# Layer 0's query, key and value products in two passes over the depth, the modulation products spread anew, gates through memory

## The chip, the cores and the metric

One core of one Trainium2 chip (trn2) runs the kernel. The metric is the device time of one execution in microseconds, from first to last instruction of the core with what lies around it. The kernel before took 1590.33 us, the median of 3 runs (1589.23 to 1595.4).

## The reference

Two blocks of layers over x, 256 tokens by 2048 (fp32). All times are those of three attention-like layers, which the kernel numbers 0, 1 and 2.

- Every layer first makes modulation vectors from a condition vector: `mod = silu(c) @ w_mod + b_mod`, split in shift, scale and gate of 2048 each. There are 11 such vectors of 2048: shift, scale, gate for layer 0; shift, scale, gate for layer 1; shift and scale for the shared keys and values; shift, scale, gate for layer 2. Each costs a matrix of 2048 by 2048, 16.8 MB, for one vector times matrix.
- Layer 0: `h = rms_norm(x) * (1 + scale) + shift`; `proj = h @ w_in` (2048 by 7168) gives q, k, v for 8 dilated attention heads, q, k, v for 4 retention heads, and gates z. The heads' output is multiplied by `silu(z)`, goes through `w_out` and is added as `x + gate * out`. An RMS norm follows.
- Layer 1: differential attention with its own q, k, v, g projection (2048 by 8192) and output projection, then `layer_norm(alpha * x + gate * y)`.
- Layer 2: keys, values and forget gates from `kv_w_2`, queries and gates from `b_w_in_2`, forgetting attention, output projection and the last layer norm.

## The kernel before

**Products.** All projections run through one frame. A chunk is 512 output columns. A step is two k-tiles (256 rows) of one chunk, 128x1024 fp32 values, 512 KB from memory; a chunk has 8 steps and a pair is two chunks, 16 steps. There are 29 pairs, 464 steps. For each step SyncE loads `raw` (four slots, line 450), ScalarE casts it to `w_hi` (line 823), VectorE subtracts to get `w_lo` (line 1120), and TensorE does three products for each k-tile and half of the tokens (lines 629 to 631: high by high, low weight by high, high weight by low), 12 matmuls of 512 columns in a step. `w_hi` and `w_lo` have four slots (LEAD): ScalarE may cast step n only when TensorE has done step n-4, and SyncE may load a slot only when `w_lo` of the step four earlier is written. A chunk accumulates in two PSUM banks, one for each half of the tokens. ScalarE copies a finished chunk out (line 844 and others) and TensorE goes on in the other two banks.

**The head.** Pairs 0 and 1 (steps 0 to 31) are special, because the activations themselves depend on modulation vectors. x is loaded, squared, scaled and turned by TensorE (line 562). Then, for each of the 16 k-tiles, VectorE makes one tile of the shift and one of the scale product (line 1134: a 128x2048 tile of the modulation matrix, 1 MB, times the condition row, summed along the row), finishes them (lines 1141, 1146), ScalarE makes `act_hi` of that k-tile (1005, 1009), VectorE `act_lo` (1153), and TensorE multiplies this one k-tile with columns 0 to 2047 of `w_in`: q and k of the dilated heads, 4 chunks in all 8 PSUM banks at once (lines 578 to 580). So each k-tile of the head uses two steps of weights (1 MB) and two modulation tiles (2 MB).

**The modulation products.** 176 tiles (11 vectors by 16), in order. GpSimd issues their loads (line 505) into a ring: 6 slots in the head (`gw` and parts of `area`), 2 slots after it. A slot is free when VectorE has used it. `MOD_STEPS` gives by hand how many tiles VectorE does in each pair after the head: 8 in each of pairs 2 to 5, then 7, 6, 3 in pairs 6, 7, 8; 4, 6, 6 in pairs 9 to 11; 5, 6, 5, 8, 8 in pairs 12 to 16; 6, 4, 6, 5, 6, 5 in pairs 17 to 22 and 4 in each of pairs 23 to 26.

**The order.** Pair 2: v of the dilated heads. Pair 3: q, k of retention; four decay tables and a lambda are made beside it (lines 1488 to 1510), from twelve small loads that SyncE issues between the weights of pair 2 (line 443). Pair 4: v of retention, and the attention steps of layer 0 begin (`ATTENTION_PAIR`), woven between steps up to pair 6. Pairs 5 and 6: the gates z, which ScalarE takes through silu and VectorE multiplies in (line 1201). Then the heads' output is turned (line 609) and pairs 7 and 8 are the output projection: VectorE multiplies each chunk by the gate row, adds it to x and takes norm statistics (lines 1214, 1219, 1223). The norm (1329 or 1331) and the next turn follow. Layer 1 has pairs 9 to 18 and layer 2 pairs 19 to 28, in the same way.

**The gate row** is the layer's gate vector on all 128 partitions. In pairs 7, 17 and 27 TensorE spreads it: 16 products of a broadcast column with the identity in 4 groups (line 598), each group copied out by ScalarE (line 906).

**Queues.** SyncE issues weights and small loads, GpSimd the modulation tiles, ScalarE bias tables and norm rows. Every engine runs its instructions in the order written; each wait holds all behind it on its engine.

## Time and profile before

| what | value |
|---|---|
| median of 3 runs | 1590.33 us |
| the profiled execution's own time | 1595.93 us |
| its span | 1594.1 us |
| mean granted TensorE clock | 0.970 |
| TensorE busy | 1461.7 us (92%) |
| VectorE busy | 1173.3 us (74%) |
| ScalarE busy | 719.0 us (45%) |
| moved by DMA | 445.68 MB, mean 280 GB/s |

The profile gives, for one execution, the busy time of each engine, groups of equal instructions, and for idle time the engine or transfer that ended it. TensorE's matmuls overlap in the pipeline, so its rate is read from starts, not from the duration of one. "Granted clock" 1.00 is 2.4 GHz and 0.50 is 1.2 GHz.

### The profile page before, as it was taken

Reading aid. Unit: us, or ns where it says so; the run is one execution under the profiler, and the core shown is the slowest. Engines: PE = TensorE matmul, PEld = TensorE weight load, DVE = VectorE, ACT = ScalarE, POOL = GpSimd, SP = SyncE. Lnnn points to the kernel's source line nnn. Section 1 sums busy time; section 2 is a strip of 40 time slices with the busy share of each in tenths; the row PEclk is TensorE's granted clock in tenths of the full one; section 3 lists DMA queues with packets and bytes.
Section 4 is the critical chain, followed back from the end, with each engine's and each line's share of the span. In section 5 each row is a group of like instructions: output and inputs, shape, how many; then the busy total and the mean of one; then the engine's idle time right before and its main releaser. Section 6 shows DMA issues by size and latency. Waiting matters only on the chain.

```text
span 1594.1 us, 19384 instructions
## 1 busy us (share of the span) xinstructions
PE 1461.7 (92%) x6730; PEld 1205.5 (76%) x6730; DVE 1173.3 (74%) x1451; ACT 719.0 (45%) x1006; POOL 112.0 (7%) x211
## 2 busy tenths in 40 slices
PE   4778999998999799999999989969999999999895
PEld 3566777787788688888887867858888778888784
DVE  5997787785778778777678867877876775556456
ACT  4345355553443444344555643434443455554431
POOL 1110000001000000000001100000000000000000
PEclk8999999999999899999999999989999999999998
DMA  9998998986968389999888869839997586655552
GB/s 386 418 416 305 360 317 331 356 289 219 326 242 299 132 310 336 319 345 325 310 277 289 264 243 339 279 118 364 321 353 277 195 294 224 205 173 164 185 187 90
DMA packets 153871, 445.68 MB, mean 280 GB/s; under 512 B 11328, under 2 KB 13632, under 8 KB 130112
## 3 DMA queue, kind: packets, MB, share of 16 engines
q1 hardware_dynamic: 125136, 249.33, 44.9%
q0 software_dynamic: 25488, 185.61, 31.8%
q10 hardware_dynamic: 3168, 9.70, 1.6%
q8 instruction: 48, 0.79, 0.2%
...
## 4 chain that ended last, share of the span: by engine, by line
PE 62%; DVE 16%; DMA 13%; ACT 5%; issue 4%; ACTq 0%; DVEq 0%; SPq 0%; POOL 0%
PE bank L629 18%; PE bank L631 18%; PE bank L630 18%; DMA raw<-in_w_in 5%; DVE gw L1134 5%; DVE w_lo L1120 4%; DMA raw<-in_a_w_out 2%; DMA gw<-in_t_ada 2%; DMA raw<-in_kv_w 2%; PE bank L747 2%; ACT w_hi L823 2%; PE bank L695 2%; PE bank L609 1%; DVE area L1134 1%; DVE w_lo L1126 1%
## 5 line engine op out<-in xcount | busy, mean ns | idle before, releaser
L823 ACT CAST w_hi<-raw 128x1024 fp32r<-128x1024 f32 x464 | 485.1, 1051 | 722.1 <-PE bank L631 415.0
L1120 DVE TENSOR_TENSOR w_lo<-raw,w_hi 128x1024 fp32r<-128x1024 f32 x428 | 517.9, 1222 | 311.9 <-ACT w_hi L823 309.5
L629 PE MATMUL bank<-w_hi,act_hi 128*128 128x512 f32 x1728 | 695.1, 402 | 14.9 <-DVE w_lo L1120 9.9
L631 PE MATMUL bank<-w_hi,act_lo 128*128 128x512 f32 x1728 | 677.2, 392 | 0.0
L630 PE MATMUL bank<-w_lo,act_hi 128*128 128x512 f32 x1728 | 676.3, 391 | 0.0
L629 PEld LDWEIGHTS bank<-w_hi,act_hi 128*128 128x128 f32 x1728 | 327.4, 189 | 88.0 <-DVE w_lo L1120 16.5
L631 PEld LDWEIGHTS bank<-w_hi,act_lo 128*128 128x128 f32 x1728 | 326.4, 189 | 70.3
L630 PEld LDWEIGHTS bank<-w_lo,act_hi 128*128 128x128 f32 x1728 | 327.4, 189 | 65.4
L1134 DVE CUSTOM_DVE_ANT_0 gw<-gw,c_act 128x2048 f32<-128x2048 f32 x156 | 356.2, 2286 | 27.5 <-DMA gw<-in_t_ada 12.4
L505 POOL DMA_DIRECT2D gw<-in_t_mod x96 | 51.1, 532 | 831.0 <-DVE products L1134 820.6
L578 PE MATMUL bank<-w_hi,act_hi 128*128 128x512 f32 x128 | 54.1, 422 | 31.1 <-DVE act_lo L1153 31.1
L578 PEld LDWEIGHTS bank<-w_hi,act_hi 128*128 128x128 f32 x128 | 25.7, 201 | 41.9 <-issue 36.8
L580 PE MATMUL bank<-w_hi,act_lo 128*128 128x512 f32 x128 | 52.6, 411 | 0.0
L579 PE MATMUL bank<-w_lo,act_hi 128*128 128x512 f32 x128 | 52.5, 410 | 0.0
L1126 DVE TENSOR_TENSOR w_lo<-raw,w_hi 128x1024 fp32r<-128x1024 f32 x36 | 43.7, 1219 | 7.2 <-ACT w_hi L823 7.2
L1134 DVE CUSTOM_DVE_ANT_0 area<-area,c_act 128x2048 f32<-128x2048 f32 x20 | 45.0, 2286 | 0.0
L944 ACT ACTIVATE probs<-probs,neg_max 128x128 f32<-128x128 f32 (+1 forms) x80 | 36.6, 458 | 17.0 <-DVE neg_max L1447 16.9
L695 PE MATMUL bank<-qk_t 128*128 128x256 f32 (+1 forms) x160 | 37.7, 343 | 0.0
L609 PE MATMUL bank<-ident,resid 128*128 128x128 f32 x96 | 15.5, 323 | 23.0 <-DVE resid L1331 12.8
L747 PE MATMUL bank<-area,probs_t 128*128 128x128 f32 (+1 forms) x208 | 33.5, 299 | 0.0
L1302 DVE TENSOR_TENSOR act_lo<-bank,act_hi 128x512 fp32r<-128x512 f32 x24 | 16.0, 689 | 22.8 <-ACT act_hi L887 22.8
L609 PEld LDWEIGHTS bank<-ident,resid 128*128 128x128 f32 x96 | 14.0, 169 | 24.8 <-DVE resid L1331 13.3
...
## 6 DMA issues: line engine op xcount, KB each, us to landing
gw<-in_t_mod POOLq DMA_DIRECT2D x96, 1024.0 KB, 7.5
raw<-in_a_w_in SPq DMA_DIRECT2D x128, 512.0 KB, 6.0
...
gw<-in_t_kv_mod POOLq DMA_DIRECT2D x32, 1024.0 KB, 7.7
...
gw<-in_t_ada POOLq DMA_DIRECT2D x28, 1024.0 KB, 8.3
area<-in_t_ada POOLq DMA_DIRECT2D x20, 1024.0 KB, 10.4
```

What stands on the lines that cost most here:

```text
L578: nc.tensor.matmul(dst, hi, w_hi[:, n % LEAD, c], start=(kt == 0), stop=False)
L579: nc.tensor.matmul(dst, hi, w_lo[:, n % LEAD, c], start=False, stop=False)
L580: last = nc.tensor.matmul(dst, lo, w_hi[:, n % LEAD, c], start=False, stop=(kt == KT - 1))
L629: nc.tensor.matmul(dst, hi, w_hi[:, b, k], start=(kt == 0), stop=False)
L630: nc.tensor.matmul(dst, hi, w_lo[:, b, k], start=False, stop=False)
L631: last = nc.tensor.matmul(dst, lo, w_hi[:, b, k], start=False, stop=(kt == KT - 1))
L695: last = nc.tensor.matmul(s_bank[:, c0:c1], q[:, tt * P:(tt + 1) * P], k[:, 0:c1 - c0], start=True, stop=(layer != 2))
L747: last = nc.tensor.matmul(o_bank[:, tt * w:(tt + 1) * w], pt[:, at:at + P], area[:, V, j, c:c + w], start=(j == 0), stop=(j == keys - 1))
L823: nc.scalar.copy(w_hi[:, b], raw[:, j % SLOTS]).then_inc(hi_ready, 1)
L1120: nc.vector.tensor_tensor(w_lo[:, j % LEAD], raw[:, j % SLOTS], w_hi[:, j % LEAD].bitcast(F32), ALU.subtract).then_inc(lo_ready, 1)
L1126: nc.vector.tensor_tensor(w_lo[:, j % LEAD], raw[:, j % SLOTS], w_hi[:, j % LEAD].bitcast(F32), ALU.subtract).then_inc(lo_ready, 1)
L1134: nc.vector.tensor_tensor_reduce(out=w, in0=w, in1=c_act[:], scale=1.0, scalar=0.0, op0=ALU.mult, op1=ALU.add, accum_out=products[:, b, k: ...
```

## The change

1. **Two passes.** The head now does k-tiles 0 to 7 only (16 steps, same four chunks in 8 banks). What it has is copied by ScalarE to `area` as partial sums. Steps 16 to 39 do k-tiles 0 to 7 of six more chunks (v of the dilated heads, v, q and k of retention), 4 steps each, their partial sums copied out too. Meanwhile VectorE makes the shift and scale tiles of k-tiles 8 to 15, two in every three steps. Steps 40 to 79 do k-tiles 8 to 15 of all ten chunks; VectorE adds each to its partial sum (`add_part`, one 128x512 instruction for each half of the tokens, in place of ScalarE's copy). The number of steps is unchanged (80 up to the end of pair 4), and so is the number of matmuls.
2. **Modulation tiles spread anew.** `PAIR_TILES` replaces `MOD_STEPS`; three slots after the head (two before), five in it (six before), and from tile 15 on three. The tiles are loaded as two halves of 4 KB in each partition (one of 8 KB before).
3. **Gates through memory.** The gate part of the modulation matrices is permuted on the host so that `mod[:, gate]` stored from SBUF is the row in order; GpSimd stores it to a DRAM tensor and ScalarE loads it back broadcast to 128 partitions. TensorE's and ScalarE's parts of the spreading are gone.
4. **Weights as one stream.** The host lays all weights out in the order of the steps, so that a step is one contiguous block with 4 KB in each partition (two rows of 2 KB before, outside the head). SyncE has one loop in place of ten.
5. Smaller: the first two weight steps are loaded before the first modulation tiles; the silu of the second condition vector moves from the start of pair 4 to pair 5, next to the silu of the gates; the small loads go with steps 32 to 43; `squares` has one buffer in place of two; `w_forget` lies in `probs`.

```diff
-GEMV_RING = 2
-HEAD_RING = 6
+GEMV_RING = 3
+HEAD_RING = 5
-MOD_STEPS = {ADA_GATE: ((2, 8), (3, 8)), A_SHIFT: ((4, 8), (5, 8)),
...
+PAIR_TILES = {3: 6, 4: 8, 5: 7, 6: 8, 7: 9, 8: 10, 9: 7, 10: 7, 11: 7, 12: 7, 13: 7, 14: 3, 15: 3, 16: 3, 17: 4,
+              18: 5, 19: 7, 20: 7, 21: 7, 22: 6, 23: 5, 24: 4, 25: 4, 26: 3}
+HALF_KT = KT // 2
+SHORT = STEPS // 2
+FIRST_PAIR = 3
+HEAD_STEPS = 2 * HALF_KT
+HEAD_TILES = 2 * KT
+FIRST_ORDER = (4, 5, 8, 9, 6, 7)
+SECOND_ORDER = (6, 7, 0, 2, 4, 1, 3, 5, 8, 9)
+SECOND_AT = HEAD_STEPS + SHORT * len(FIRST_ORDER)
+FRONT_STEPS = SECOND_AT + SHORT * len(SECOND_ORDER)
+    if pair == 5:
+        return [(at, first + i) for i, at in enumerate((0, 2, 9, 10, 12, 13, 15))]
+    return [(1 + i * (13 / n), first + i) for i in range(n)]
+        def row_slot(g):
+            return g % HEAD_RING if g < 3 * HEAD_RING else g % GEMV_RING
...
         @block.sync
-            sp.wait_ge(gw_landed[0], 16)
+            for k in range(FRONT_STEPS):
+                if k == 2:
+                    sp.wait_ge(gw_landed[1], 16)
+                wait(sp, lo_ready, k - SLOTS + 1)
+                load_step(k * P, k)
+                if 0 <= k - SMALLS_AT < SMALLS:
+                    small_load(k - SMALLS_AT)
...
+            with sp.Fori(0, WEIGHT_CHUNKS) as i:
                 for j in range(STEPS):
+                    k = FRONT_STEPS + j
+                    sp.wait_ge(lo_ready, i * STEPS + (k - SLOTS + 1))
+                    load_step(i * (STEPS * P) + k * P, j)
...
         @block.gpsimd
+                if b - 1 in GATES and k == GEMV_RING - 1:
+                    store_gate(GATES.index(b - 1))
+            def store_gate(layer):
+                pool.wait_ge(mod_ready, GATES[layer] - 1)
+                pool.dma_start(gate_rows[layer].rearrange("(p k) -> p k", p=P), mod[:, GATES[layer]]
+                               ).then_inc(gate_stored, 16)
+            pool.wait_ge(raw_landed[1], 16)
...
         @block.tensor
-            def spread_gate(layer, n):
...
+            def short(n):
+                q, kt0, m, j = short_of(n)
+                if j == 0 and kt0 == 0:
+                    pe.wait_ge(parted, 2 * (m + 1) if m < 2 else 8 + 2 * (m - 1))
+                elif j == 0 and m < 2:
+                    pe.wait_ge(parted, 8 + 2 * (len(FIRST_ORDER) - 1 + m))
+                elif j == 0:
+                    pe.wait_ge(evacuated, 2 * (m - 1))
+                if kt0 and m == 0:
+                    pe.wait_ge(head_hi, kt0 + STEP_KT * (j + 1))
+                    pe.wait_ge(head_lo, kt0 + STEP_KT * (j + 1))
+                pe.wait_ge(lo_ready, n + 1)
...
         @block.scalar
-            def gate_row(layer, n):
-                act.wait_ge(t_ready, T[("gate", layer, n)] + 1)
-                nc.scalar.copy(area[:, K, 0, n * CHUNK:(n + 1) * CHUNK], t_bank[:]).then_inc(t_free, 1)
+            def gate_rows_of(layer):
+                act.wait_ge(weighed, OUT0[layer] + OUTS[layer])
+                act.wait_ge(gate_stored, 16 * (layer + 1))
+                act.dma_start(area[:, K, 0], row_of(gate_rows[layer])).then_inc(gate_landed, 16)
+            def keep_part(n):
...
+                for q in chunks:
+                    act.wait_ge(half_used, n + 1)
...
+                    for tt in range(TT):
...
+                        nc.scalar.activation(part(q, tt), bank[:], ACT.Copy, scale=part_scale(q)).then_inc(parted, 1)
         @block.vector
+            def add_part(n):
+                q, kt0, place, j = short_of(n)
+                if not kt0 or j < SHORT - 1:
+                    return
+                dve.wait_ge(half_used, n + 1)
+                for tt in range(TT):
...
+                    nc.vector.scalar_tensor_tensor(out=dst, in0=bank, scalar=part_scale(q), in1=first, op0=ALU.mult,
+                                                   op1=ALU.add).then_inc(evacuated, 1)
+            def front():
+                for m in range(HEAD_STEPS, FRONT_STEPS + LEAD):
+                    n = m - LEAD
...
+                    split_low(m, m % LEAD)
+                    kt, late = divmod(m - HEAD_STEPS, 3)
+                    if kt < HALF_KT and late < 2:
+                        gemv_step(2 * (HALF_KT + kt) + late)
+                        if late:
+                            head_finish(HALF_KT + kt)
+                    if late == 2 and 0 <= kt - 1 < HALF_KT:
+                        head_low(HALF_KT + kt - 1)
```

## Rows read from the trace of the kernel before

**Rows 1.** The page's first part: busy time, share, instructions.
```profile
PE 1461.7 (92%) x6730; PEld 1205.5 (76%) x6730; DVE 1173.3 (74%) x1451; ACT 719.0 (45%) x1006; POOL 112.0 (7%) x211
```

**Rows 2.** Busy time by stretch; then clock, DMA share, GB/s; first busy (x) is PE.
```profile
29.00:171.80 142.80, 119.55 (x480) 94.00 (x481) 127.58 (x150) 61.48 (x78) 14.78 (x28) 0.95 0.96 373
171.80:308.20 136.40, 125.94 (x545) 100.40 (x545) 108.39 (x133) 67.99 (x92) 12.12 (x23) 0.96 0.94 350
...
434.00:545.00 111.00, 100.77 (x464) 84.38 (x462) 82.19 (x93) 42.39 (x50) 5.46 (x10) 0.93 0.73 258
...
765.00:934.00 169.00, 165.03 (x778) 136.24 (x776) 131.79 (x223) 95.28 (x186) 18.57 (x34) 0.99 0.83 282
```

**Rows 3.** Busy time by stretch: steady products, and part of the head.
```profile
600.00:740.00 140.00, 140.00 (x619) 115.95 (x619) 106.69 (x93) 59.68 (x64) 10.03 (x19) 1.00 0.93 328
100.00:120.00 20.00, 16.22 (x64) 12.61 (x63) 19.60 (x25) 8.46 (x11) 2.81 (x6) 0.91 1.02 417
```

**Rows 4.** PE's waits: whole run, then 171.8 to 308.2 us. Total, times, longest.
```profile
PE bank L578 <- DVE act_lo L1153: 31.1, 15, 8.0
...
PE bank L629 <- DVE w_lo L1120: 8.4, 9, 2.6
```

**Rows 5.** Timeline of DVE, one k-tile of the head (start, duration).
```profile
34.73 1.22 DVE L1126 TENSOR_TENSOR w_lo<-raw,w_hi 128x1024 fp32r<-128x1024 f32 x1
...
36.40 1.22 DVE L1126 TENSOR_TENSOR w_lo<-raw,w_hi 128x1024 fp32r<-128x1024 f32 x1
37.53 2.28 DVE L1134 CUSTOM_DVE_ANT_0 area<-area,c_act 128x2048 f32<-128x2048 f32 x1
...
39.74 2.29 DVE L1134 CUSTOM_DVE_ANT_0 area<-area,c_act 128x2048 f32<-128x2048 f32 x1
...
42.35 1.22 DVE L1126 TENSOR_TENSOR w_lo<-raw,w_hi 128x1024 fp32r<-128x1024 f32 x1
```

**Rows 6.** Timeline, start of the head: SyncE's, ScalarE's and TensorE's rows.
```profile
14.62 1.85 SPq L461 DMA_DIRECT2D raw<-in_w_in  x4
...
26.30 1.04 ACT L823 CAST w_hi<-raw 128x1024 fp32r<-128x1024 f32 x1 [2.62 <-DMA raw<-in_w_in]
...
29.16 0.76 PE L578 MATMUL bank<-w_hi,act_hi 128*128 128x512 f32 x1 [7.98 <-DVE act_lo L1153]
```

**Rows 7.** DVE's groups, 171.8 to 308.2 us: busy, mean ns, idle before and releasers.
```profile
L1120 DVE TENSOR_TENSOR w_lo<-raw,w_hi 128x1024 fp32r<-128x1024 f32 x42 | 50.6, 1221 | 16.9 <-ACT w_hi L823 16.8
L1134 DVE CUSTOM_DVE_ANT_0 gw<-gw,c_act 128x2048 f32<-128x2048 f32 x22 | 50.4, 2290 | 13.6 <-DMA gw<-in_t_ada 11.0 <-DMA gw<-in_t_mod 2.6
```

**Rows 8.** DVE's groups, 487.4 to 541 us (pair 8 and norm).
```profile
L1219 DVE SCALAR_TENSOR_TENSOR resid<-resid,side 128x512 f32<-128x512 f32 x6 | 3.8, 683 | 0.0
```

**Rows 9.** Timeline of PE: two of the twelve gate groups, and the one that waited.
```profile
457.45 1.05 PE L598 MATMUL bank<-ident,mod 128*128 128x128 f32 x8
...
461.08 1.05 PE L598 MATMUL bank<-ident,mod 128*128 128x128 f32 x8
...
972.77 1.13 PE L598 MATMUL bank<-ident,mod 128*128 128x128 f32 x8 [1.63 <-ACT area L906]
```

**Rows 10.** Timeline of PE: first turns after norm 0, layer 1's gating, norm 1.
```profile
541.26 3.68 PE L609 MATMUL bank<-ident,resid 128*128 128x128 f32 x16 [10.17 <-DVE resid L1329]
...
940.78 3.67 PE L609 MATMUL bank<-ident,area 128*128 128x128 f32 x16 [6.87 <-DVE area L1201]
...
1053.05 3.68 PE L609 MATMUL bank<-ident,resid 128*128 128x128 f32 x16 [12.84 <-DVE resid L1331]
```

**Rows 11.** Timeline of ACT: the casts before those two waits of layer 1.
```profile
935.09 1.04 ACT L823 CAST w_hi<-raw 128x1024 fp32r<-128x1024 f32 x1 [5.47 <-DMA raw<-in_a_w_out]
...
1043.04 1.04 ACT L823 CAST w_hi<-raw 128x1024 fp32r<-128x1024 f32 x1 [4.41 <-DMA raw<-in_kv_w]
```

**Rows 12.** DMA issues of the page: KB each, median us to landing.
```profile
gw<-in_t_mod POOLq DMA_DIRECT2D x96, 1024.0 KB, 7.5
...
area<-in_final_gain ACTq DMA_DIRECT2D x1, 1024.0 KB, 8.0
```

More of the change, by code:

```diff
@@ L93, with short_of @@
 VECS = VEC_FINAL + 3 * KT
+GATES = (ADA_GATE, A_GATE, B_GATE)
 def gemv_steps(pair):
-    for b, steps in MOD_STEPS.items():
-        k = 0
-        for p, n in steps:
-            if p == pair:
-                first = 1
-                return [(first + i * ((14 - first) / n), b, k + i) for i in range(n)]
-            k += n
-    return []
+    n = PAIR_TILES.get(pair, 0)
+    first = HEAD_TILES + sum(k for p, k in PAIR_TILES.items() if p < pair)
+    if pair == 5:
+        return [(at, first + i) for i, at in enumerate((0, 2, 9, 10, 12, 13, 15))]
+    return [(1 + i * (13 / n), first + i) for i in range(n)]
+def short_of(n):
+    if n < SECOND_AT:
+        m, j = divmod(n - HEAD_STEPS, SHORT)
+        return FIRST_ORDER[m], 0, m, j
+    m, j = divmod(n - SECOND_AT, SHORT)
+    return SECOND_ORDER[m], HALF_KT, m, j
 def alibi(n):
@@ L159, in t_uses @@
                         uses.append(("probs", layer, s - 2))
-                if pair == OUT_PAIR[layer] and h < 4:
-                    uses.append(("gate", layer, h))
+                if pair == OUT_PAIR[layer] and h == 0:
+                    uses.append(("end", layer))
         if pair == FORGET_PAIR:
             uses += [("forget_rows",), ("forget",)]
-    return {u: n for n, u in enumerate(uses)}
+    count = {}
+    n = 0
+    for u in uses:
+        count[u] = n
+        n += u[0] != "end"
+    return count
 def two_blocks(nc, a, out):
@@ L530, in loads_after @@
                 for h in range(PAIR_STEPS):
-                    for at, b, k in steps:
-                        if h <= at < h + 1 and KT * b + k + GEMV_RING < MODS * KT:
-                            load(KT * b + k + GEMV_RING)
+                    for at, g in steps:
+                        if h <= at < h + 1 and g + GEMV_RING < MODS * KT:
+                            load(g + GEMV_RING)
                     if steps_of(pair, h):
@@ L780, in _ @@
             head()
-            first_pair()
-            pairs(3, 1)
+            for n in range(HEAD_STEPS, PAIR_STEPS * ATTENTION_PAIR[0]):
+                short(n)
             attention_pair(4)
@@ L966, in values_step @@
                     for tt in range(TT):
-                        nc.scalar.activation(squares[:, tt],
+                        wait(act, squared, TT * HEAD_ROOTS["head", layer, u] + tt)
+                        nc.scalar.activation(squares[:],
                                              o_bank[:, tt * WIDE:(tt + 1) * WIDE], ACT.Square,
@@ L1176, in head @@
                     head_keep(r)
-                for kt in range(KT):
+                for kt in range(HALF_KT):
                     split_low(2 * kt, 2 * kt % LEAD)
@@ L1513, in _ @@
             head()
-            for n in range(LEAD):
-                split_low(HEAD_STEPS + n, n)
-            for p in range(FIRST_PAIR, 5):
-                pair(p)
+            front()
             pair(5, gate_y(0))
@@ new lines, in weight_steps @@
+def weight_steps(inputs):
+    w_in = np.asarray(inputs["w_in"])[0]
+    out = np.empty((FRONT_STEPS + WEIGHT_CHUNKS * STEPS, P, STEP_KT * CHUNK), np.float32)
+    head = w_in[:HALF_KT * P, :4 * CHUNK].reshape(HALF_KT, P, 2, 2 * CHUNK)
+    out[:HEAD_STEPS] = head.transpose(0, 2, 1, 3).reshape(HEAD_STEPS, P, 2 * CHUNK)
+    for n in range(HEAD_STEPS, FRONT_STEPS):
+        q, kt0, _, j = short_of(n)
+        row, col = (kt0 + STEP_KT * j) * P, q * CHUNK + (0 if q < 6 else 2 * D - 6 * CHUNK)
+        step = w_in[row:row + STEP_KT * P, col:col + CHUNK].reshape(STEP_KT, P, CHUNK)
+        out[n] = step.transpose(1, 0, 2).reshape(P, STEP_KT * CHUNK)
+    at = FRONT_STEPS
+    for name, col, chunks in WEIGHT_RUNS:
+        w = np.asarray(inputs[name]).reshape(D, -1)[:, col:col + chunks * CHUNK]
+        w = w.reshape(STEPS, STEP_KT, P, chunks, CHUNK).transpose(3, 0, 2, 1, 4)
+        out[at:at + chunks * STEPS] = w.reshape(chunks * STEPS, P, STEP_KT * CHUNK)
+        at += chunks * STEPS
+    return out.reshape(-1, STEP_KT * CHUNK)
```

305 lines of the change are left out of this document (157 added, 148 removed).

## The prediction, made before the changed kernel ran

> **What bounds the kernel now.** I read the page's busy times first [rows 1]: TensorE works 92% of the span, so the kernel is near TensorE's own time and a gain must come from its idle time (132 us), from a low clock, or from work taken off it. Then busy time by stretch. Undisturbed, TensorE does 619 matmuls in 140.00 us [rows 3]: 0.2262 us each, 2.71 us for a step of 12, 21.7 us for a chunk, with VectorE at 76% and the DMA engines at 0.93. The stretches show where it is not so [rows 2]. From 29.0 to 171.8 us it does the first 40 steps, 480 matmuls, in 142.8 us; alone they take 108.6. From 171.8 to 308.2 us it does the next 40 (with 65 small products of attention) in 136.4 us and idles for 10.5.
>
> Third, what ends the waits. In the head it is `act_lo`, fifteen times, 31.1 us [rows 4], and `act_lo` is late because VectorE is full: 19.60 of 20 us [rows 3]. One k-tile takes VectorE from 34.73 to 42.35 us, 7.62 us [rows 5]: two splits of weights (1.13 us from start to start), two modulation products (2.21 us) and small work, where TensorE needs 5.4. The DMA engines are full too, 417 GB/s at share 1.02. Between 171.8 and 308.2 us it is `w_lo` that is late [rows 4], and VectorE itself waits there, 16.8 us for casts and 13.6 us for modulation tiles not yet landed [rows 7], at DMA share 0.94 and only 350 GB/s. So the head is bound by VectorE and DMA together, the stretch behind it by late transfers, and the rest by TensorE but for short waits at turns and norms [rows 10].
>
> **The change part by part**, from the profiled execution's own 1595.9 us.
>
> *Start.* The first weights are issued at 14.62 us, after the first modulation tile; the second cast waits 2.62 us for them, and the first product of the head comes at 29.16 us [rows 6]. Now two weight steps are issued at the beginning. Bounds: nothing (the 1 MB tiles then land later) and the whole wait with the one before it, some 4 us. Nearest is the wait seen: -3 us.
>
> *Steps 0 to 39.* Products and splits are the same in number, 32 and 40, but all 40 steps now share the products. VectorE needs 16 x 7.62 = 121.9 us and 8 more splits x 1.13 = 9.0: 130.9 us, in place of 142.8. In the new stage three steps cost it 8.75 us and TensorE 8.1, so VectorE still leads, narrowly. Transfers: 373 GB/s x 142.8 us = 53.3 MB [rows 2] at the head's 417 GB/s are 127.8 us, so VectorE binds, narrowly again. The copies of partial sums are ScalarE's, busy for 61 of 143 us. Bounds: 0 (the rate of the next stretch, below) and -15 (transfers alone). With some unevenness: -10 us.
>
> A rule against this part: the Trainium skill, page "DMA: Bandwidth & Descriptors", section "Where 436 GB/s comes from", says that for transfers from HBM the HBM side, about 358 GB/s a core, is what binds. By it 53.3 MB would take 149 us and the part would give nothing. The trace disagrees, with 417 GB/s in the head [rows 3].
>
> *Steps 40 to 79.* Here 14 modulation tiles are left of 22. TensorE's work is 136.4 less 10.5 us idle less 4% of clock (0.96, 5.5 us) = 120.4 us. Transfers fall from 350 x 136.4 = 47.7 MB by 8 MB to 39.3 MB, 319 GB/s, under the 328 at which TensorE never idled [rows 3]. VectorE takes over the ten chunks' sums, 20 x 0.683 = 13.7 us by the nearest instruction [rows 8]; with 40 splits (45.2), 14 products (30.9) and its other work (108.4 - 50.6 - 50.4 = 7.4) that is 97 us of 120: hidden. Without that cover it would cost its 13.7 us. What is late next: the first attention steps and the table work, 3 us by guess from two waits over 1 us left. Bounds 0 and -16: -13 us.
>
> *Gates.* Two groups start at 457.45 and 461.08 us [rows 9], 3.63 us apart with a step of 2.71 between: 0.92 us a group, 12 groups, 11.0 us, and the wait of 1.63: -12.7 us, all on TensorE. The new row is a broadcast load of 1 MB on ScalarE's queue like the gain row, which lands in 8.0 us [rows 12]; it is issued at the end of pair 6 and wanted a turn and a chunk (over 21.7 us) later. GpSimd's store waits for `mod_ready` with tile loads queued behind it, but just after VectorE has finished that vector. Both at nothing; if late, the add of the first chunk of pair 7 waits.
>
> *Pairs 7 and 8* now have 9 and 10 tiles for 6 and 3. In the first chunk of pair 8 lie six: VectorE needs 8 x 1.13 + 6 x 2.21 + 6 x 0.683 = 26.4 us against 21.7, and transfers of 18.9 MB in 43.4 us would be 435 GB/s. So it comes 4.7 us late to its last sum, and norm 0, which all wait for, moves by what is not caught up. Room there is in the time before, with DMA share 0.73 [rows 2]. Bounds 0 and +10: +3 us.
>
> *Layer 1.* Pairs 14 to 16 have 9 tiles for 21. TensorE idles 4.0 us of 765 to 934 at clock 0.99 [rows 2]: -2. The turn after the gating waits 6.87 us, norm 1 12.84 where norm 0 waits 10.17 [rows 10]; before both a cast was held 5.47 and 4.41 us by weights [rows 11]. Lighter pairs and weights in 4 KB pieces should bring them earlier: -2.5 each. Bounds 0 and -13.
>
> *At nothing:* the moved silu (ScalarE has room, and the waits at pair 4 are counted above), single `squares`, small loads (same steps), more tiles in pairs 9 to 13 (7 x 2.21 + 16 x 1.13 = 33.6 of 43.4 us), pairs 5 and 6, all of layer 2 (bounds +3 and -5).
>
> Sum: -3 - 10 - 13 - 12.7 + 3 - 7 = -42.7, so 1553.2 us for a profiled execution. This one was 5.6 us above the median of its kind; against the median it is 1547.6, rounded 1548.
>
> **Rivals.**
> - *Transfers stay slow.* The stretch behind the head moved 350 GB/s at share 0.94, 372 at a full share. If the 4 KB halves of the modulation tiles fare like that, 53.3 MB take 143 us and steps 0 to 39 give nothing: 1558. For: nothing shows 4 KB alone. Against: the head's weights have 4 KB rows already and run within the 417. The skill's 358 GB/s (same page and section) would be this case, a little worse. 0.14.
> - *Pairs 7 and 8 clog.* Both queues at 435 GB/s is above anything seen; if weights come late too, TensorE loses what VectorE does: +8 more, 1556. 0.14.
> - *The waits of steps 40 to 79 stay.* They are then the order on ScalarE and VectorE (table loads, the lambda, sums now in the way) and not transfers: 1561. Against: 13.6 us of VectorE's waits name modulation tiles [rows 7]. 0.08.
> - *The change doesn't do what it says*: all three together and no gain at the start and in layer 1, so that the gates' -12.7 stand against +3 and +8 in pairs 7 and 8: 1589. 0.04.
> - *Slower: weights late behind deeper modulation.* With three slots one more tile of 1 MB can stand in front of each weight step, 2.5 us at 417 GB/s. In pairs 9 to 13 and 19 to 21, now 7 tiles each, TensorE never idled, but share was 0.93. If its 128 steps each lost 0.5 us, 64 us: 1612. It decides from 0.33 us a step (42.7/128). Against: only 328 GB/s are asked there, a tile lands in 7.5 us [rows 12] and is used every 6.2, so seldom is more than one or two under way. 0.04.
>
> Of that last rival the Trainium skill, same page, section "Queues, rings and completion order", says that each DMA engine takes turns between queues packet by packet; smaller pieces of modulation tiles would then leave weights a larger share. No row here separates it.
>
> **How the numbers follow.** The forecast has 0.56. Its own range is 1536 to 1558. For 8 in 10 I take the good ends of start, steps 0 to 79 and layer 1 (-4 - 15 - 16 - 12.7 - 13 = -60.7, 1530) and on the other side two of the rivals together (1548 + 10 + 13 = 1571): 1528 to 1572. A measurement of this kernel can tell about 0.5%, 8 us, from no change. Faster: forecast and the first three rivals, 0.92. Same: 0.04. Slower: 0.04.
>
> **What would show it.** First product of the head near 26 us. Step 40 begins near 159 us and step 80 near 282 (171.8 and 308.2 before), the new stage at about 8.8 us for three steps with DMA near 415 GB/s. No `w_lo` waits over 1 us between them beyond two or three. The projection chunks of pairs 7, 17, 27 shorter by 3.7 us. Norm 0's wait of 10 to 15 us, norm 1's near 10, layer 1's gating near 4. It is wrong if the share is 1.0 at 370 GB/s in the front, if TensorE idles in pairs 9 to 13, or if norm 0's wait passes 20 us.

## The result, and the profile after

The changed kernel takes 1574.46 us (median of 4 runs, 1571.09 to 1577.23), the one before 1592.87 (4 runs, 1589.23 to 1596.68): ratio 0.988, 95% interval 0.985 to 0.991. So it is faster by 18 us, where 42 were forecast, and 2 us outside the range. The profiled executions differ by 21.4 us (1574.56 and 1595.93); the steps below are held against these. Of the kernels tried below, weights2k has one slow execution (a lower granted clock, 1605 us, and it is the profiled one) and respread two; the ratios leave these out, and without them the medians are 1588.5 and 1577.9 us.

The page's first part after, to set beside [rows 1]:

```profile
PE 1444.3 (92%) x6634; PEld 1190.2 (76%) x6634; DVE 1183.0 (75%) x1471; ACT 710.8 (45%) x992; POOL 113.4 (7%) x214
```

TensorE has 96 matmuls fewer (the gates' twelve groups of eight, [rows 9], are gone) and is busy 17 us less, VectorE 10 us more (the sums of the halves). Busy time by stretch, the columns as in [rows 2]: the first 40 steps, the next 40, chunks 15 and 16 (pairs 7 and 8), chunk 17 with norm 0, and chunks 39 to 41 (pairs 19 and 20):

```profile
27.80:157.60 129.80, 115.58 (x480) 92.16 (x481) 122.79 (x145) 64.57 (x88) 15.64 (x28) 0.97 1.00 402
157.60:277.90 120.30, 118.63 (x545) 97.82 (x545) 101.22 (x137) 60.23 (x81) 7.43 (x14) 1.00 0.89 326
435.40:482.50 47.10, 44.98 (x194) 35.61 (x192) 43.94 (x45) 16.34 (x16) 4.77 (x9) 1.00 0.93 359
482.50:528.10 45.60, 26.57 (x113) 20.95 (x113) 40.58 (x49) 13.48 (x17) 4.42 (x8) 0.85 0.87 347
1052.20:1129.50 77.30, 70.31 (x290) 55.96 (x289) 62.85 (x55) 29.16 (x31) 6.36 (x12) 0.96 0.89 334
```

The front does what it should: 142.6 us became 129.8 and 136.4 became 120.3, and between steps 40 and 79 TensorE idles 1.7 us of 120.3. The third and fourth row are new: there VectorE is at 93% and 89% and the DMA engines at 0.93 and 0.87, and two chunks last 47.1 us where 43.5 are needed. The turns of [rows 10] after, from the timeline of TensorE (idle time before in brackets), with the three longest of the waits inside pairs 7, 8 and 20:

```profile
498.26 0.50 PE L674 MATMUL bank<-w_hi,act_hi 128*128 128x512 f32 x1 [2.94 <-DVE w_lo L1187]
...
523.93 3.68 PE L654 MATMUL bank<-ident,resid 128*128 128x128 f32 x16 [13.84 <-DVE resid L1439]
...
919.71 3.29 PE L654 MATMUL bank<-ident,area 128*128 128x128 f32 x16 [4.50 <-DVE area L1318]
...
1023.44 3.67 PE L654 MATMUL bank<-ident,resid 128*128 128x128 f32 x16 [10.11 <-DVE resid L1441]
...
1100.14 0.50 PE L674 MATMUL bank<-w_hi,act_hi 128*128 128x512 f32 x1 [1.89 <-DVE w_lo L1187]
1125.07 0.80 PE L674 MATMUL bank<-w_hi,act_hi 128*128 128x512 f32 x1 [3.99 <-DVE w_lo L1187]
```

Norm 0's wait grew from 10.17 to 13.84 us, which is 3.7 of the 9.4 us that chunk 17 lost; in the rest of that chunk TensorE idles 5 us more and is busy 1 us more. Layer 1's gating wait fell from 6.87 to 4.50, norm 1's from 12.84 to 10.11.

Where the time went shows best in the length of each chunk. The table is worked out: the start of every 96th product of TensorE's timeline (eight steps of twelve), and the difference to the next. Bare, a chunk is 21.7 us; chunk 17 holds norm 0 and its turn, and chunks 28 to 33 attention.

| chunks | before | after | light_loads | light_vector | light_both | rear |
|---|---|---|---|---|---|---|
| 15, 16 (pairs 7, 8) | 43.7 | 47.1 | 44.8 | 46.5 | 43.5 | 48.8 |
| 17 (pair 8, norm 0) | 36.2 | 45.6 | 43.8 | 45.8 | 36.3 | 44.9 |
| 38 to 41 (pairs 19, 20) | 89.6 | 101.9 | 90.9 | 91.4 | 89.8 | 90.9 |
| lead over before at chunk 10 | | 30.3 | 30.3 | 29.6 | 30.8 | 29.3 |
| lead at chunk 18 | | 17.3 | 26.8 | 18.8 | 34.2 | 17.9 |
| lead at chunk 42 | | 17.3 | 30.0 | 16.6 | 40.1 | 25.6 |

After 80 steps the changed kernel leads by 30.3 us. It loses 5.0 in pairs 5 and 6, the gates give 4.9 in the first chunk of pair 7, and so it leads by 30.1 at chunk 15; at the end of pair 8 by 17.3. Pairs 14 to 18 bring it to 29.6, and pairs 19 and 20 take it back to 17.3.

### The profile page after: what moved, and what is told of

Same layout as the page of the kernel before. It is cut to its first block, busy times and chain, and to the rows that moved or that the text cites. A ratio compares the mean times of both kernels' runs of the same rounds, so it can differ in the third digit from the quotient of the medians.

```text
span 1572.7 us, 19098 instructions
## 1 busy us (share of the span) xinstructions
PE 1444.3 (92%) x6634; PEld 1190.2 (76%) x6634; DVE 1183.0 (75%) x1471; ACT 710.8 (45%) x992; POOL 113.4 (7%) x214
## 3 DMA queue, kind: packets, MB, share of 16 engines
q1 hardware_dynamic: 69840, 249.33, 43.5%
## 4 chain that ended last, share of the span: by engine, by line
PE 51%; DVE 20%; DMA 16%; issue 6%; ACT 6%; ACTq 0%; DVEq 0%; SPq 0%; POOL 0%
DMA raw<-in_t_steps 13%; PE bank L674 13%; PE bank L676 13%; PE bank L675 13%; DVE gw L1201 8%; DVE w_lo L1187 5%; ACT w_hi L873 3%; PE bank L797 2%; DVE w_lo L1193 2%; PE bank L745 2%; PE bank L640 1%; PE bank L642 1%; PE bank L641 1%; PE bank L654 1%; DMA gw<-in_t_mod 1%
## 5 line engine op out<-in xcount | busy, mean ns | idle before, releaser
L676 PE MATMUL bank<-w_hi,act_lo 128*128 128x512 f32 x1536 | 602.0, 392 | 0.0
L675 PE MATMUL bank<-w_lo,act_hi 128*128 128x512 f32 x1536 | 601.2, 391 | 0.0
L1201 DVE CUSTOM_DVE_ANT_0 gw<-gw,c_act 128x2048 f32<-128x2048 f32 x170 | 388.3, 2285 | 5.0 <-DMA gw<-in_t_ada 3.5
L674 PEld LDWEIGHTS bank<-w_hi,act_hi 128*128 128x128 f32 x1536 | 290.6, 189 | 86.2 <-DVE w_lo L1187 21.4
L676 PEld LDWEIGHTS bank<-w_hi,act_lo 128*128 128x128 f32 x1536 | 290.1, 189 | 62.6
L675 PEld LDWEIGHTS bank<-w_lo,act_hi 128*128 128x128 f32 x1536 | 290.7, 189 | 58.1
L1193 DVE TENSOR_TENSOR w_lo<-raw,w_hi 128x1024 fp32r<-128x1024 f32 x84 | 102.1, 1222 | 25.6 <-ACT w_hi L873 25.4
L529 POOL DMA_DIRECT2D gw<-in_t_mod x96 | 51.5, 536 | 696.9 <-DVE products L1201 690.7
L642 PE MATMUL bank<-w_hi,act_lo 128*128 128x512 f32 x256 | 99.8, 390 | 0.0
L641 PE MATMUL bank<-w_lo,act_hi 128*128 128x512 f32 x256 | 99.7, 390 | 0.0
L640 PEld LDWEIGHTS bank<-w_hi,act_hi 128*128 128x128 f32 x256 | 48.1, 188 | 19.1 <-issue 4.1
L642 PEld LDWEIGHTS bank<-w_hi,act_lo 128*128 128x128 f32 x256 | 48.0, 188 | 10.1
L641 PEld LDWEIGHTS bank<-w_lo,act_hi 128*128 128x128 f32 x256 | 48.1, 188 | 9.6
L614 PE MATMUL bank<-w_hi,act_hi 128*128 128x512 f32 x64 | 27.2, 425 | 16.6 <-DVE act_lo L1221 16.6
L529 POOL DMA_DIRECT2D gw<-in_t_ada x42 | 22.6, 539 | 224.4 <-DVE products L1201 212.8
L654 PE MATMUL bank<-ident,resid 128*128 128x128 f32 x96 | 15.8, 327 | 24.0 <-DVE resid L1439 13.8
```

Source lines behind the costliest of these rows:

```text
L529: pool.dma_start(dst, src[row + k * P:row + (k + 1) * P].rearrange("p (t n) -> p t n", t=TT)).then_inc(landed, 16)
L640: nc.tensor.matmul(dst, hi, w_hi[:, n % LEAD, k], start=(kt == kt0), stop=False)
L641: nc.tensor.matmul(dst, hi, w_lo[:, n % LEAD, k], start=False, stop=False)
L642: last = nc.tensor.matmul(dst, lo, w_hi[:, n % LEAD, k], start=False, stop=(kt == kt0 + HALF_KT - 1))
L674: nc.tensor.matmul(dst, hi, w_hi[:, b, k], start=(kt == 0), stop=False)
L675: nc.tensor.matmul(dst, hi, w_lo[:, b, k], start=False, stop=False)
```

## The experiments

Two theories stood at first. A: in those pairs the queue of modulation tiles is backlogged (loads wait in it all the time), and weights get too small a share of the DMA engines. The casts of ScalarE, in pair 8 of the changed kernel:

```profile
483.43 1.06 ACT L873 CAST w_hi<-raw 128x1024 fp32r<-128x1024 f32 x1 [5.49 <-DMA raw<-in_t_steps]
487.25 1.05 ACT L873 CAST w_hi<-raw 128x1024 fp32r<-128x1024 f32 x1 [2.77 <-DMA raw<-in_t_steps]
491.05 1.06 ACT L873 CAST w_hi<-raw 128x1024 fp32r<-128x1024 f32 x1 [2.75 <-DMA raw<-in_t_steps]
494.83 1.05 ACT L873 CAST w_hi<-raw 128x1024 fp32r<-128x1024 f32 x1 [2.72 <-DMA raw<-in_t_steps]
498.58 1.05 ACT L873 CAST w_hi<-raw 128x1024 fp32r<-128x1024 f32 x1 [2.70 <-DMA raw<-in_t_steps]
```

One step every 3.8 us, and TensorE uses one every 2.71. B: VectorE is full in pairs 7 and 8 (16 subtractions, 9 or 10 tiles, the sums).

**light_loads** and **light_vector** take one of the two away, for the tiles of pairs 7, 8, 19 and 20.

```diff
+LIGHT = {g for p in (7, 8, 19, 20) for _, g in gemv_steps(p)}
 # light_loads
+                cols = 128 if g in LIGHT else 1024
-                pool.dma_start(dst, src[...].rearrange("p (t n) -> p t n", t=TT)
+                pool.dma_start(dst[:, :, 0:cols], src[...].rearrange("p (t n) -> p t n", t=TT)[:, :, 0:cols]
 # light_vector
+                cols = 128 if g in LIGHT else 1024
+                w = w[:, :, 0:cols]
...
```

> The changed kernel, but the 33 modulation tiles of pairs 7, 8, 19 and 20 are loaded over an eighth of their columns (1 KB of 8 KB a partition); VectorE still reduces all columns, so the modulation values are not the reference's. Theory A (a step of weights lands every 3.77 us instead of within TensorE's 2.71 us while the modulation queue is backlogged, since its 8 KB packets take two turns' worth of bytes for each 4 KB weight packet): chunks 15 to 17 go back from 23.7, 23.4 and 45.6 us to the 21.9, 21.8 and 36.2 of the kernel before, and chunks 38 to 41 from 24.6, 23.4, 24.5 and 29.3 to 23.9, 21.8, 22.0 and 21.9: some 20 us in all, 1553 us. Theory B (VectorE is full in these pairs): nothing moves, 1574 us, and the 29.3 us of chunk 41 stays. Theory C (both, each alone enough): under 5 us gained.

> The changed kernel, but VectorE reduces the tiles of pairs 7, 8, 19 and 20 over 256 of their 2048 columns (about 0.3 us each in place of 2.21); all loads as they are, so the modulation values are not the reference's. Theory A (weights late by the modulation queue's packets): a slot comes free 1.9 us sooner, the transfers are the same bytes, chunks 15 to 17 keep their loss: within 5 us of 1574 us, except that chunk 41 (four norm row instructions beside it) may gain. Theory B (VectorE full): some 20 us gained, 1553 us, with chunks 15 to 17 at 21.9, 21.8 and 36.2 us and chunks 38 to 41 near 22 us each.

light_loads: 1564.98 us (ratio 0.982, 0.979 to 0.984); light_vector: 1571.38 (0.984, 0.981 to 0.987). Neither theory holds alone. In pairs 19 and 20 either relief returns all but 1 to 2 of the 12.3 us. In pairs 7 and 8 neither does: over chunks 15 to 17 light_loads returns 4.1 us of the 12.8 and light_vector 0.4. (Another 5.4 us of light_loads' lead at chunk 18 were there at chunk 15 already, where kernels with the same code up to pair 8 differ by 2.7.) The stretches say why; light_loads, chunks 15 and 16, then 17:

```profile
430.00:474.80 44.80, 44.23 (x194) 35.91 (x193) 44.80 (x46) 16.85 (x16) 6.37 (x9) 1.00 0.67 214
474.80:518.60 43.80, 27.35 (x114) 22.12 (x112) 39.05 (x49) 12.43 (x16) 5.20 (x8) 0.81 0.62 227
```

With the DMA engines at 0.67, VectorE is busy 44.80 us of 44.80. And light_vector:

```profile
434.30:480.80 46.50, 44.20 (x194) 35.91 (x193) 29.43 (x46) 16.13 (x16) 4.75 (x9) 1.00 0.93 367
480.80:526.60 45.80, 26.40 (x113) 20.86 (x111) 26.58 (x47) 13.38 (x17) 3.88 (x7) 0.79 0.82 334
```

With VectorE at 63% the DMA engines stay at 0.93, and norm 0 waits longer than in the changed kernel, since VectorE's sums stand in its order behind the low halves of steps ahead, which wait for their weights (TensorE's last product of pair 8 ends at 505.5 us, the sums begin at 514.63):

```profile
509.73 1.23 DVE L1190 TENSOR_TENSOR w_lo<-raw,w_hi 128x1024 fp32r<-128x1024 f32 x1 [2.44 <-ACT w_hi L876]
513.49 1.23 DVE L1190 TENSOR_TENSOR w_lo<-raw,w_hi 128x1024 fp32r<-128x1024 f32 x1 [2.54 <-ACT w_hi L876]
514.63 1.28 DVE L1336 TENSOR_TENSOR side<-bank,area 128x512 f32<-128x512 f32 x2
...
522.49 3.68 PE L657 MATMUL bank<-ident,resid 128*128 128x128 f32 x16 [16.96 <-DVE resid L1444]
```

So theory D: pairs 7 and 8 have two bounds, one behind the other. **light_both** takes both edits.

> Light loads and light VectorE work at once, for the tiles of pairs 7, 8, 19 and 20 (an eighth of their columns loaded and reduced; the modulation values are not the reference's). Theory D (in pair 8 VectorE's 10 tiles, 16 subtractions and sums fill it, and apart from that the DMA engines are full too, so that relieving one leaves the other; in pairs 19 and 20 the loss needs both and either relief is enough): chunks 15 to 17 last 21.8, 21.8 and 36.2 us where light_loads had 23.0, 21.8 and 43.8 and light_vector 21.8, 24.7 and 45.8; chunks 38 to 41 stay at the 91 us of each alone. 1573 - 13 - 11 - 3 = 1546 us. Rival E (the sums or the gating rows themselves hold pair 8, not the tiles): chunk 17 stays above 42 us, 1556 us.

1551.6 us (ratio 0.973, 0.970 to 0.975). Chunks 15 and 16 are bare products, and norm 0 waits 10.17 us as before:

```profile
431.40:474.90 43.50, 43.50 (x193) 36.05 (x192) 29.49 (x47) 16.82 (x16) 6.39 (x9) 1.00 0.71 223
474.90:511.20 36.30, 25.41 (x114) 21.12 (x112) 25.22 (x45) 12.45 (x16) 4.49 (x7) 0.86 0.66 245
```

Theory D holds: in chunks 15 to 17 the two edits return 12.9 us together, and 4.1 and 0.4 alone. The whole is 5.6 us over what was expected, and chunks 19 to 21 (in pairs 9 and 10, with seven tiles each) lost 5 us of it: 71.0 for 65.9. That is not the light tiles' doing. By the same starts these chunks last 65.3 us as bare products, 65.9 in the changed kernel and 67.9 in rear, but 72.0 in light_loads, 73.8 in light_vector, 72.4 in respread, 72.6 in rows_later and 73.2 in ring2. In old_spread, with four tiles in pair 9 and six in pair 10, they last 65.3. So seven tiles there are at the edge of what comes in on time: in these three chunks the longest wait of a cast for its weights is 7.2 us in light_vector and 4.5 in the changed kernel. What tips a kernel over that edge no run here tells, nor whether the changed kernel's other executions stay on the good side. It also means that the totals of light_loads and light_vector are too small a measure of the reliefs: light_vector gained 1.4 us by chunk 18 and 10.5 in pairs 19 and 20, and lost 12.7 against the changed kernel in the chunks between.

**packets4k** and **weights2k** ask what sets the share of the weights.

```diff
 # packets4k
-        gw = sb("gw", [P, GEMV_RING, D])
+        gw = sb("gw", [P, TT, GEMV_RING, 1024])
 # weights2k
-        raw = sb("raw", [P, SLOTS, STEP_KT, CHUNK])
+        raw = sb("raw", [P, STEP_KT, SLOTS, CHUNK])
```

> The changed kernel, with the three modulation buffers laid out so that the two halves of a tile's row are not neighbours in SBUF: each 8 KB packet becomes two of 4 KB, as the weights' are; nothing else differs. Theory A (shares go by packets taken in turn): while the modulation queue is backlogged weights get 1/2 of 417 GB/s, a step each 2.5 us, which is under TensorE's 2.71: the 2.7 us waits of ScalarE's casts for DMA go, and most of the loss of pairs 7, 8, 19 and 20 is back: 1556 us, 1552 to 1564. Theory B (VectorE full): 1574 us. If shares don't go by packets, a backlogged step still lands every 3.77 us and the time is 1574 us.

> The changed kernel with the raw weight buffers laid out so that a step's two 2 KB halves are not neighbours: weights move in 2 KB packets again, as in the kernel before, and nothing else differs. If each packet takes a turn whatever its size, a step under a modulation backlog now gets a fifth of 417 GB/s and lands every 6.3 us instead of 3.77: chunks 15 to 17, 40 and 41 and the front lose 10 us each at least, 1600 us or more. If the share goes by bytes or by something else (packets4k left it at 64% for modulation), the intervals stay near 3.8 us and only the cost of smaller packets shows: 1574 to 1582 us. This also tells what the one stream of weights is worth in the change.

packets4k: 1570.97 us (0.986, 0.983 to 0.990), no different from the changed kernel. weights2k: 1589.03 (0.996, 0.994 to 0.999), some 14 us slower than it. The queues over 16 us in pair 8 (packets, MB, share of the engines; q0 carries modulation tiles, q1 weights), 483 to 499 us of the changed kernel:

```profile
DMA packets 1250, 6.58 MB, mean 411 GB/s; under 512 B 137, under 2 KB 137, under 8 KB 759
...
q0 software_dynamic: 553, 4.01, 62.1%
q1 hardware_dynamic: 696, 2.55, 39.1%
```

packets4k, 487 to 503 us:

```profile
q0 software_dynamic: 1052, 4.07, 65.5%
q1 hardware_dynamic: 616, 2.26, 35.1%
```

weights2k, 497 to 513 us:

```profile
q0 software_dynamic: 545, 3.94, 59.9%
q1 hardware_dynamic: 1338, 2.58, 42.4%
```

The modulation queue takes 61, 64 and 60% of the bytes, whichever side's packets are halved. A stretch of 16 us one chunk earlier (451 to 467, 455 to 471 and 465 to 481 us) gives 63, 61 and 63%, so the differences are those between stretches. A turn for each packet would have given 50% in packets4k and 80% in weights2k, so that part of theory A falls. What 2 KB packets cost is rather engine time: 42.4% of the engines' time for 2.58 MB, where 4 KB packets took 39.1% for 2.55, some 7% more for a byte. That they cost the 14 us in this way is argued. Where they cost it isn't shown either: in weights2k's profile the first 40 steps take 140.6 us for 129.8 and chunk 17 52.3 for 45.6, but that is the execution of 1605 us.

**ring2** undoes the third buffer.

```diff
-GEMV_RING = 3
-HEAD_RING = 5
+GEMV_RING = 2
+HEAD_RING = 4
```

> The changed kernel with two modulation buffers instead of three (and four instead of five in the front). Theory D: the ring's depth only moves when a tile lands; with two, fewer bytes stand before the weights in pairs 15 to 17 and 38 to 41, but VectorE waits for tiles itself: 0 to 8 us slower, 1574 to 1582. Rival F (the third buffer is what makes weights late): pairs 7, 8, 19 and 20 give back over half of their 25 us and the time is 1562 us or less unless the front loses it.

1604.59 us (1.007, 1.004 to 1.009): 30 us slower than with three. In its profile (1612.9 us, the longest of five) the front loses 17 (chunk 10 begins at 295.3 us for 277.9), chunks 14 to 17 take 135.1 us for 116.4, and only chunks 38 to 41 are shorter, 98.8 for 101.9. In pairs 7 and 8 the third buffer doesn't cause the loss, it makes it smaller; rival F falls, and I had put its price at a quarter of what it is.

**respread** and **rear** spread the same tiles otherwise, **pair20** moves three and **old_spread** goes back to the old numbers from pair 9 on.

```diff
-PAIR_TILES = {3: 6, 4: 8, 5: 7, 6: 8, 7: 9, 8: 10, ... 11: 7, 12: 7, 13: 7, 14: 3, 15: 3, 16: 3, 17: 4, 18: 5, 19: 7, 20: 7, 21: 7, ...}
+pair20:       11: 8, 12: 8, 13: 8, 20: 4
+respread:     3: 8, 5: 9, 6: 9, 7: 7, 8: 7, 14: 5, 15: 5, 16: 5, 19: 6, 20: 3, 21: 6; C_AT (5, 1)
+rear:         14: 5, 15: 5, 16: 5, 19: 6, 20: 3, 21: 6
+old_spread:   9: 4, 10: 6, 11: 6, 12: 5, 13: 6, 14: 5, 15: 8, 16: 8, 17: 6, 18: 4, 19: 6, 20: 5, 21: 6, 22: 5, 23: 4, 26: 4
```

> The changed kernel with three tiles of pair 20 moved to pairs 11, 12 and 13 (8, 8, 8 in place of 7, 7, 7, and 4 in place of 7). Theory A (weights late): pair 20 asks for less and chunks 40 and 41 come back from 24.5 and 29.3 us to near 22 each: 8 us gained, 1566 us; pairs 11 to 13 ask for 8 tiles (16.8 MB in 43.4 us, 387 GB/s of 417) and lose 0 to 4. Theory B (VectorE full with 16 subtractions, 7 tiles and 4 norm row instructions): pair 20 falls from 42.7 to 36.1 us of VectorE work: 8 us gained as well, and pairs 11 to 13 (16 x 1.13 + 8 x 2.21 = 35.8 us of 43.4) lose nothing. What tells them apart is pairs 11 to 13.

> The changed kernel with the same tiles spread otherwise: pairs 3 to 8 hold 8, 8, 9, 9, 7, 7 (6, 8, 7, 8, 9, 10 before), with silu of the second c at the start of pair 5, and pairs 14 to 22 hold 5, 5, 5, 4, 5, 6, 3, 6, 6 (3, 3, 3, 4, 5, 7, 7, 7, 6 before); 9 to 13 stay at 7. Theory D: pair 8 asks VectorE for 16 x 1.13 + 7 x 2.21 + 8 x 0.68 = 39 us of 43.4 and the DMA engines for 362 GB/s; chunks 15 to 17 come back to 82 us from 92.7, chunks 38 to 41 to 91 from 102, and 2 to 4 us are lost in pairs 3 to 6 and 14 to 16: 1574 - 10.7 - 11 + 3 = 1555 us. If pairs 5 and 6 have no room (their turn already came 7 us late), 1562 us.

> The changed kernel with one part undone: from pair 9 on the modulation tiles are spread as in the kernel before (4, 6, 6, 5, 6, 5, 8, 8, 6, 4, 6, 5, 6, 5, 4, 4, 4, 4 for pairs 9 to 26). By the leads of the changed kernel over the one before (pairs 14 to 16 and the gating wait gained 5.1 us, norm 1 2.8, pairs 9 to 13 lost 0.9, pairs 19 and 20 lost 12.3) the new spread lost some 5 us in all: chunks 38 to 41 back to 91 us from 102, chunks 28 to 33 longer by up to 5: 1566 to 1572 us. If what was gained in pairs 14 to 18 was not the spread's but the 4 KB weights', all of the 11 us: 1563.

> A version meant to beat both: the changed kernel with pairs 3 to 13 as they are and pairs 14 to 22 at 5, 5, 5, 4, 5, 6, 3, 6, 6 tiles, so that the pair with the four norm row instructions (20) has three and the attention pairs, whose DMA share is 0.67, take six more. VectorE's work in pair 20 falls to 16 x 1.13 + 3 x 2.21 + 4 x 2.28 = 33.8 us of 43.4. Chunks 38 to 41 92.3 us as in respread, pairs 14 to 16 at most 2 longer: 1574 - 9.6 + 2 = 1566 us.

pair20: 1573.18 us (0.988, 0.985 to 0.990). Chunks 38 to 41 take 92.8 us for 101.9, as expected. The first two of its pairs of eight tiles, chunks 22 to 25, lose 0.3 us; chunk 27, the end of the third, and chunk 28 behind it lose 3.6, and 30 another 0.9. VectorE has 35.8 us of work for 43.4 in such a pair, and in chunk 27 the DMA engines are at 0.99, so there it is most likely they:

```profile
724.10:747.80 23.70, 22.66 (x97) 17.76 (x96) 19.57 (x17) 9.40 (x10) 2.58 (x5) 1.00 0.99 394
```

respread: 1579.74 (0.989, 0.987 to 0.992). Its rear gained 9.6 us (92.3 for 101.9), its pair 8 4 us (chunk 17: 41.8), but pairs 3 to 6 lost 8.5 (chunk 10 at 282.1 us, chunk 14 at 420.2 for 411.7) and chunks 19 to 21 another 6.5: there is no room ahead of pair 7 either. old_spread: 1571.62 (0.987, 0.984 to 0.989); chunks 38 to 41 take 93.0, but chunk 33 takes 35.2 for 32.5, 35 27.0 for 22.8. From chunk 18 to 42 it takes 601.8 us and the changed kernel 601.4: the new spread from pair 9 on gave in layer 1 what it took in layer 2. rear: 1568.43 (0.986, 0.983 to 0.989), 6 us under the changed kernel by the medians, with intervals that overlap; in its profile pairs 19 and 20 take 90.9 us:

```profile
1030.30:1121.20 90.90, 90.26 (x401) 74.09 (x402) 76.64 (x75) 39.66 (x47) 4.82 (x9) 0.99 0.74 271
```

What filled pair 20 is in VectorE's timeline of the changed kernel: between two subtractions, where one is wanted every 2.71 us, lie 5.66 us with the two instructions of a norm row.

```profile
1093.21 1.22 DVE L1187 TENSOR_TENSOR w_lo<-raw,w_hi 128x1024 fp32r<-128x1024 f32 x1
1094.34 2.28 DVE L1453 TENSOR_TENSOR resid<-resid,area 128x2048 f32<-128x2048 f32 x1
1096.66 2.29 DVE L1454 TENSOR_TENSOR resid<-resid,area 128x2048 f32<-128x2048 f32 x1
1098.87 1.22 DVE L1187 TENSOR_TENSOR w_lo<-raw,w_hi 128x1024 fp32r<-128x1024 f32 x1
```

So three things meet in pair 20: seven tiles to load, seven to reduce, and the norm rows. Relieving either the loads or the reductions was enough.

**gates_alone** and **stream_alone** make one part of the change in the kernel before.

```diff
 # gates_alone, in the kernel before
-                        if p in OUT_PAIR and c == 0 and j >= 4:
-                            spread_gate(OUT_PAIR.index(p), j - 4)
...
+                act.dma_start(area[:, K, 0], row_of(gate_rows[layer])).then_inc(gate_landed, 16)
 # stream_alone, in the kernel before
-                    sp.dma_start(raw[:, j % SLOTS], src[:, j * STEP_KT:(j + 1) * STEP_KT, bass.ds(col, CHUNK)]
+                    sp.dma_start(raw[:, j % SLOTS].rearrange("p c n -> p (c n)"), w_steps[bass.ds(col + j * P, P), :]
```

> The kernel before with one part of the change alone: the gate row goes through memory and comes back as one broadcast load; the 48 small products and 12 copies are gone. By the prediction's step 12.7 us less on TensorE, and by the first chunks of pairs 7, 17 and 27 in the changed kernel (4.8, 5.3 and 3.6 us shorter) 13.7: 1593.5 - 13 = 1580.5 us. If the row's 1 MB load costs what it moves (2.5 us at 417 GB/s, beside the gain row and the bias loads at the turn), 3 to 7 us of it come back in the chunks behind the turns: 1584 to 1588.

> The kernel before with one part of the change alone: all weights in one array in the order of their steps, 4 KB a partition at a time, where 432 of 464 steps came as two 2 KB pieces. Theory G (2 KB packets cost DMA time wherever the engines are full; the changed kernel with 2 KB packets was 15 us slower): the stretch behind the head (171.8 to 308.2 us, share 0.94 at 350 GB/s) shortens by 5 us or more, pairs 14 to 17 by 2 to 5: 1580 to 1586 us. Theory H (only the changed kernel is dense enough to need it): under 4 us, 1590 us or more.

gates_alone: 1585.44 us (0.995, 0.993 to 0.997), 7 us gained. Pairs 7 and 27 gave their 3.7 and 2.9, but pair 17 took 52.2 us for 51.5: its first chunk 24.5 for 29.5, its second 27.7 for 21.9. stream_alone: 1591.33 (0.999, 0.997 to 1.001), theory H: alone, next to nothing, though in the changed kernel the same thing is worth some 14 us. (Its profile is 6.1 us ahead over chunks 28 to 37, as theory G had it for pairs 14 to 17, and 2.0 behind over 38 to 41; twelve runs show no such gain.)

**gates_no_row** and **rows_later** ask whether the row loads, 3 MB at once in pair 17, are what took it.

```diff
 # gates_no_row, from gates_alone
-                act.dma_start(area[:, K, 0], row_of(gate_rows[layer]))
+                act.dma_start(area[:, K, 0, 0:64], row_of(gate_rows[layer, 0:64]))
 # rows_later, from rear: norm_rows(0) moved behind turn_scaled(2, ...), norm_rows(1) behind pair(0, 17, None)
```

> The kernel before with the gates through memory alone, and of the gate row only 64 of 2048 columns loaded (so most of the gate row is not the reference's). Gates alone gained 7.1 us where 12.7 were counted; in its profile the second chunk of pair 17 lasts 27.7 us for 21.9, after 3.15 MB of row loads were issued within 1 us. Theory K (the row's own 1 MB load, together with the gain and shift rows, makes weights late): that chunk is back under 24 us and the time is 1580.5 us. Rival L (the rest of the gates' gain went elsewhere, for instance into weights late whatever the row does): 1585 us.

> Another version meant to beat both: rear, with the gain row of layer 0 loaded at the start of pair 9 in place of the end of pair 6, and the gain and shift rows of layer 1 after pair 17 in place of before it, so that the gate rows are loaded alone. Theory K: 1 MB less in pair 7 (2.5 us of the DMA engines there) and 2 MB less in pair 17: 2 to 5 us less than rear, 1564 to 1566 us. Rival L: as rear, 1568, or slower if pair 9, 10 or 18 can't take the rows.

gates_no_row: 1586.31 us (0.996, 0.994 to 0.998), no faster than with the load, and the second chunk of pair 17 still takes 26.3; the second of pair 7 took 26.3 as well, for 21.8 in gates_alone. Theory K falls. That chunk, gates_no_row:

```profile
961.70:988.00 26.30, 23.60 (x97) 19.07 (x96) 21.92 (x23) 8.40 (x8) 2.12 (x4) 0.94 0.90 334
```

The same chunk before, behind a first chunk 5 us longer:

```profile
973.60:995.50 21.90, 21.90 (x99) 18.15 (x98) 18.35 (x19) 6.91 (x7) 1.58 (x3) 1.00 0.84 302
```

Two MB of other rows, six tiles and the weights have to come in either way; the 5 us in which TensorE spread gates had been cover for them. That is an argument from these rows, since no run took the other rows away. rows_later: 1571.91 (0.985, 0.982 to 0.988), its interval holding both a gain and a loss against rear; in its profile (1581.67 us, the longest of six) chunk 17 took 49.6 us. It decides nothing.

## Why the prediction was wrong, step by step

- *Start*, -3: measured -1.4 (first product at 27.77 us for 29.16). The tiles then land later, as the lower bound had it: the second tile's product starts at 19.44 us for 17.84.
- *Steps 0 to 39*, -10: measured -12.8 (142.6 to 129.8), VectorE at 95%. The rival "Transfers stay slow" falls: 402 GB/s at share 1.00. The Trainium skill, page "DMA: Bandwidth & Descriptors", section "Where 436 GB/s comes from", has about 358 GB/s as what binds; the trace disagrees again.
- *Steps 40 to 79*, -13: measured -16.1, the good end of the bounds. That fits with late transfers as the cause of the waits, as argued; no run tells which part of the change ended them (stream_alone leads by 0.2 us there).
- *Gates*, -12.7: the first chunks of pairs 7, 17 and 27 are 4.9, 5.4 and 3.5 us shorter, 13.8. The step was right in the changed kernel, but alone in the kernel before it is worth 7. In the changed kernel pair 17 keeps its gain because it and the pairs before it have fewer tiles: it takes 47.0 us for 51.5, where gates_alone takes 52.2, and old_spread, the changed kernel with the old tiles, 51.5 again.
- *Layer 1*, -7: measured -5.1 by the end of the gating wait and -2.8 at norm 1, less 0.9 lost in pairs 9 to 13. old_spread tells the two apart: with the old tiles the attention and its gating wait gain 0.5 us of the 5.1 (lead 20.3 at chunk 28, 20.8 at chunk 34), so those were the lighter pairs'; norm 1's 2.9 stay, so they were not. Which part brought those stays open.
- *Pairs 7 and 8*, +3 of 0 to 10: measured +12.8 behind the first chunk, the rival "Pairs 7 and 8 clog". **This step failed.** I had both loads right, VectorE 26.4 us for 21.7 and transfers of 435 GB/s, and then set them against "room", the DMA share of 0.73 over 434 to 545 us. That mean holds a norm. Parted at the end of chunk 16, the kernel before has 0.86 in the chunks of bare products and 0.62 in the chunk with the norm:

```profile
465.50:509.20 43.70, 43.70 (x196) 36.18 (x195) 36.59 (x38) 16.85 (x17) 2.51 (x5) 1.00 0.86 305
509.20:545.40 36.20, 25.57 (x113) 21.09 (x112) 25.80 (x36) 12.38 (x16) 1.36 (x3) 0.86 0.62 211
```

So the room for catching up was not there, and 435 GB/s is above the 402 to 418 of the fullest stretches. light_both shows the price of the two together: 12.9 us, over the step's upper bound of 10. The prediction's sign of this, norm 0's wait over 20 us, didn't show, since 13.84 is inside its 10 to 15: most of the loss lay in waits for `w_lo` among the products.

- *At nothing, layer 2*, +3 to -5: measured +12.3 in pairs 19 and 20. **This step failed too.** The 33.6 us of VectorE's work in a pair of seven tiles left out the norm rows of pair 20, 4 x 2.28 = 9.1 us, so that it was 42.7 of 43.4. A full VectorE is half of the cause: light_vector, which relieves it alone, returns 10.5 us, but so does light_loads, which leaves it full and relieves the transfers (10.9). rear and pair20, with four and three tiles fewer in pair 20, return 11.0 and 9.1.
- *At nothing, pairs 5 and 6*: measured +5.0 (lead 30.3 to 25.3), but kernels with the same code up to there lost 1.4, 2.2 and 2.0 (old_spread, rear, pair20), so half of it is scatter between executions.
- *At nothing, pairs 9 to 13*: measured +0.9, and that is in part luck. With the same seven tiles in pairs 9 and 10, six other kernels lost 5 to 8 us more in chunks 19 to 21 (light_both, above).
- The slower rival (weights late behind deeper modulation) came true in its mechanism in pairs 7, 8, 19 and 20, and in other kernels in pairs 9 and 10; but ring2 shows that depth is not to blame.

Sum of what was measured: -1.4 - 12.8 - 16.1 + 5.0 - 13.8 + 12.8 + 0.9 - 7.9 + 12.3 = -21.0, of 21.4. The gains were 6 us larger than forecast and the losses 28. The larger gains made up for part of the losses, so the total is nearer the forecast than its steps are. My reading of the whole, which no single run shows: what the front saved was 30 us of TensorE waiting; the 48 tiles that had to be loaded and reduced by the end of pair 8 stayed the same, and with less waiting to lie in they filled VectorE and the DMA engines together.
